# The MoE output product as three split products, with the low half of w2 made on GpSimd

## The reference

```
def expert_block(args):
    xb, e = args
    return (jax.nn.silu(xb @ exp_w1[e]) * (xb @ exp_w3[e])) @ exp_w2[e]
```

## Time and profile before

| | |
|---|---|
| time, median of 3 | 3186.52 us (3183.03 to 3187.85) |
| the profiled execution | 3187.85 us, its span 3185.8 us |
| busy over the span | PE 88%, PEld 59%, DVE 43%, ACT 33%, POOL 18% |
| stage 6 | from about 2215 us to the end |
| output product L2072 | 736 records, 323.6 us busy |
| hidden products L2042 | 2208 records, five groups, 904.8 us busy |
| low parts of w1 and w3, L1850 | 256 on VectorE, 296.2 us busy |
| high parts of w1 and w3, L1909 | 256 on ScalarE, 248.9 us busy |

### The profile page before, as it was taken

How to read it: one execution, slowest core, us unless ns; L and a number is a source line. 1 busy time by engine, 2 the same in 40 slices (tenths; PEclk the granted TensorE clock), 3 DMA queues, 4 the chain that set the end, 5 groups by cost and what they waited for, 6 DMA issues and landing times. The chain is left out here.

```text
span 3185.8 us, 38331 instructions
## 1 busy us (share of the span) xinstructions
PE 2792.0 (88%) x11587; PEld 1871.8 (59%) x11588; DVE 1355.5 (43%) x2342; ACT 1049.3 (33%) x2001; POOL 578.5 (18%) x1206
## 2 busy tenths in 40 slices
PE   5985999999949777797999999981799999999998
PEld 1334644444435554556899999971566666666655
DVE  4655375221203232233255444521465465544564
ACT  3226121111112212122255555420444454433452
POOL 0000011000000000005145455554121121211232
PEclk9995999999979888895599999975899999999999
DMA  7455111121178787854011111101687698666694
GB/s 293 145 138 183 29 42 40 40 66 36 31 191 238 182 205 181 209 124 128 17 59 61 63 53 53 49 34 46 229 307 233 199 342 286 230 224 201 216 327 132
DMA packets 305306, 466.75 MB, mean 147 GB/s; under 512 B 27048, under 2 KB 193600, under 8 KB 298336
## 3 DMA queue, kind: packets, MB, share of 16 engines
q1 hardware_dynamic: 223410, 384.14, 38.1%
q0 software_dynamic: 16976, 39.52, 5.5%
q10 hardware_dynamic: 64832, 41.96, 4.7%
HBM read 367.33 MB, written 113.81 MB: 151 GB/s over the span
## 5 line engine op out<-in xcount | busy, mean ns | idle before, releaser
L748 PE MATMUL ps_proj<-sb_hT,sb_win 128*128 128x512 f32 x768 | 335.5, 596 | 7.6 <-DVE sb_rot L837 6.0
L2072 PE MATMUL ps_byp<-sb_w,sb_gT 128*128 128x512 f32 x736 | 323.6, 592 | 0.7 <-ACT sb_gT L1926 0.7
L2042 PE MATMUL ps_bh<-sb_w,sb_bxTh 128*128 128x512 f32 x736 | 295.4, 401 | 0.0
L748 PEld LDWEIGHTS ps_proj<-sb_hT,sb_win 128*128 128x128 f32 x768 | 145.6, 191 | 189.5 <-issue 182.6
L2072 PEld LDWEIGHTS ps_byp<-sb_w,sb_gT 128*128 128x128 f32 x736 | 136.2, 190 | 154.9 <-issue 154.0
L1620 DVE CUSTOM_DVE_ANT_0 sb_pr<-ps_S,sb_mask 128x640 f32<-128x640 f32 x128 | 105.6, 825 | 216.4 <-PE ps_S L1469 216.3
L1138 DVE TENSOR_TENSOR sb_ab<-sb_ab,ps_prod 128x512 f32<-128x512 f32 x64 | 44.1, 689 | 358.5 <-ACT sb_ab L1114 358.5
L2042 PE MATMUL ps_bh<-sb_w1h,sb_bxTh 128*128 128x512 f32 x368 | 164.0, 446 | 26.0 <-DVE sb_w L1850 17.3
L1489 PE MATMUL ps_O<-sb_v,sb_pt 128*128 128x64 f32 (+1 forms) x1280 | 175.9, 293 | 0.0
L1489 PEld LDWEIGHTS ps_O<-sb_v,sb_pt 128*128 128x128 f32 x1280 | 173.2, 214 | 0.0
L1341 POOL MEMSET sb_pr<- 128x1026 int32 x1 | 1.0, 958 | 909.5 <-POOLq L185 909.5
(11 more groups left out here) (274 smaller groups left out, 5179.4 us busy)
## 6 DMA issues: line engine op xcount, KB each, us to landing
sb_raw_w<-in_exp_w SPq DMA_DIRECT2D x60, 2048.0 KB, 13.0
sb_w<-in_exp_w SPq DMA_DIRECT2D x30, 2048.0 KB, 8.1
sb_ada<-in_ada_w SPq DMA_DIRECT2D x16, 1536.0 KB, 7.4
scr_filt<-sb_fout ACTq DMA_DIRECT2D x128, 128.0 KB, 2.5
sb_yh<-scr_filt SPq DMA_DIRECT2D x32, 512.0 KB, 11.1
scr_hy_y<-sb_sp SPq DMA_DIRECT2D x32, 512.0 KB, 11.5
sb_yx<-scr_hy_y SPq DMA_DIRECT2D x32, 512.0 KB, 7.9
scr_hy_v<-sb_yx SPq DMA_DIRECT2D x64, 256.0 KB, 4.2
```

The source lines that it names most:

```text
L748: ins = pe.matmul(mp[:, (NQ + n) % 4, :], w[:, pc % 3, k, (ct % 2) * P:(ct % 2 + 1) * P], g.hT[:, k, c * 512:(c + 1) * 512], start=(k == 0 ...
L2042: ins = pe.matmul(out, a[:, k, :], b(k), start=(k == 0 and j == 0), stop=(k == n - 1 and j == 2))
L2072: ins = pe.matmul(yp[:, half, :], gT[:, k, :], w2[par][:, k, cs], start=(k == 0), stop=(k == FT - 1))
```

## The change

The output product takes the split form too.

- w2 is loaded into a raw tile. Two casts of 128x2048 on ScalarE (`high2`) make its high part `w2h`, behind Silu in each first block. Two subtractions of 128x2048 on GpSimd make the low part, written over the raw one, between the scatter and the gather of a first block.
- The gated tile is cast to its high part `gTh` on ScalarE (`gated_high`, where the copy was), and VectorE subtracts to get the low part (`gated_low`), ahead of its gating multiplication.
- TensorE's `output` calls `split_product`: 24 products in place of 8. It waits for the low parts instead of the copy and the load.
- To make room, the high part of w3 is in one buffer instead of two. ScalarE therefore waits, ahead of its casts for a first block, until the hidden products of the block before are done.

```diff
-        w2 = [e.sb(st, f"w2_{b}", [P, FT, D]) for b in range(2)]
+        raw2, w2 = zip(*[raw_and_low(f"w2_{b}", [P, FT, D]) for b in range(2)])
-        w3h = [e.sb(st, f"w3h_{b}", [P, KT, FH], F32R) for b in range(2)]
+        w3h = e.sb(st, "w3h", [P, KT, FH], F32R)
+        w2h = [e.sb(st, f"w2h_{b}", [P, FT, D], F32R) for b in range(2)]
...
@@ VectorE
+            def gated_low(n):
+                ve.wait_ge(ghi, n)
+                ve.tensor_tensor(cols(gT), cols(gp), cols(gTh).bitcast(F32), ALU.subtract).then_inc(glo, 1)
+
             def body(n, ex, par, half, first):
                 if first:
                     low13(ex, par, 1)
+                if not starts(n):
+                    gated_low(n)
...
@@ ScalarE
+            def high2(par, half):
+                act.wait_ge(ldw2[par], 16 * (half + 1))
+                for part in range(2):
+                    cs = slice(part * (FT * D // 2), (part + 1) * (FT * D // 2))
+                    act.copy(cols(w2h[par])[:, cs], cols(raw2[par])[:, cs]).then_inc(hi2, 1)
...
                 if first:
+                    if not starts(n):
+                        act.wait_ge(hm, 2 * n + 1)
                     high13(ex, par, half, 1)
...
                 act.activation(sg[:, :], hp[:, 0, :], ACT.Silu).then_inc(sgd, 1)
+                if first:
+                    high2(par, half)
                 turned(n + 1)
...
@@ GpSimd
                 scatter(n)
+                if first:
+                    for part in range(2):
+                        pool.wait_ge(hi2, 2 * ex + part + 1)
+                        pool.sem_inc(passed, 1)
+                        cs = slice(part * (FT * D // 2), (part + 1) * (FT * D // 2))
+                        pool.tensor_tensor(cols(w2[par])[:, cs], cols(raw2[par])[:, cs],
+                                           cols(w2h[par])[:, cs].bitcast(F32), ALU.subtract).then_inc(lo2, 1)
                 gather(n + 2)
...
@@ TensorE
-                pe.wait_ge(gtc, n + 1)
+                pe.wait_ge(glo, n + 1)
...
-                    for k in range(FT):
-                        ins = pe.matmul(yp[:, half, :], gT[:, k, :], w2[par][:, k, cs], start=(k == 0), stop=(k == FT - 1))
-                    ins.then_inc(ym, 1)
+                    split_product(yp[:, half, :], gTh, gT, lambda k: w2h[par][:, k, cs], lambda k: w2[par][:, k, cs], FT)\
+                        .then_inc(ym, 1)
...
-                    if first:
-                        pe.wait_ge(ldw2[1 - par], 16 * (half + par))
-                    else:
-                        pe.wait_ge(ldw2[par], 16 * (half + 1))
+                    pe.wait_ge(lo2, 2 * ex if first else 2 * ex + 2)
```

More of the change, by code:

```diff
@@ L1736, in stage6 @@
         sg = e.sb(st, "sg", [P, FH])
-        gT = e.sb(st, "gT", [P, FT, P])
+        gT = e.sb(st, "gT", [P, FT, P], F32R)
+        gTh = e.sb(st, "gTh", [P, FT, P], F32R)
         y = e.sb(st, "by", [P, D])
@@ L1749, in stage6 @@
         lo13 = e.sem("s6_w13_low")
+        hi2 = e.sem("s6_w2_high")
+        lo2 = e.sem("s6_w2_low")
         rl = e.sem("s6_records_loaded")
@@ L1761, in stage6 @@
         gtt = e.sem("s6_gated_turned")
-        gtc = e.sem("s6_gated_turned_copied")
+        ghi = e.sem("s6_gated_high")
+        glo = e.sem("s6_gated_low")
         ym = e.sem("s6_output_product")
@@ L1808, in high @@
         def high(par, m):
-            return w3h[par] if m else w1h[par]
+            return w3h if m else w1h[par]
         def cols(t, m=None):
@@ L1820, in load2 @@
             src = i["exp_w2"][0, bass.ds(ex, 1)].rearrange("a (k p) f -> p (a k) f", p=P)
-            eng.dma_start(w2[par][:, :, :], src).then_inc(ldw2[par], 16)
+            eng.dma_start(raw2[par][:, :, :], src).then_inc(ldw2[par], 16)
         @block.vector
@@ L1843, in _ @@
             ve.tensor_copy(info[:, 1, :], inf[:, 1, :]).then_inc(cnt, 1)
+            ve.sem_inc(glo, 1)
             def low13(ex, par, m):
@@ L1900, in _ @@
             total = experts(ve, body)
+            gated_low(total)
             output(total)
@@ L1922, in turned, with gated_high @@
                 act.copy(cols(xTh)[:, 512:], cols(xf)).then_inc(xhi, 1)
-            def gated_copied(n):
+            def gated_high(n):
                 act.wait_ge(gtt, n)
-                act.copy(cols(gT), cols(gp)).then_inc(gtc, 1)
+                act.copy(cols(gTh), cols(gp)).then_inc(ghi, 1)
             def body(n, ex, par, half, first):
@@ L1930, in body @@
                 if first:
+                    if not starts(n):
+                        act.wait_ge(hm, 2 * n + 1)
                     high13(ex, par, half, 1)
                 if not starts(n):
-                    gated_copied(n)
+                    gated_high(n)
                     act.wait_ge(gd, n)
@@ L1951, in _ @@
             total = experts(act, body)
-            gated_copied(total)
+            gated_high(total)
         @block.gpsimd
@@ L2059, in turn_gated @@
                 pe.wait_ge(gd, n)
-                pe.wait_ge(gtc, n)
+                pe.wait_ge(glo, n)
                 for f in range(FT):
@@ L2087, in body @@
                 if not starts(n):
-                    if first:
-                        pe.wait_ge(ldw2[1 - par], 16 * (half + par))
-                    else:
-                        pe.wait_ge(ldw2[par], 16 * (half + 1))
+                    pe.wait_ge(lo2, 2 * ex if first else 2 * ex + 2)
                     pe.sem_inc(passed_t, 1)
                     output(n, 1 - par if first else par)
-            for s in (hm, ym, gtc):
+            for s in (hm, ym):
                 pe.sem_inc(s, 1)
@@ L2099, in _ @@
             turn_gated(total)
-            pe.wait_ge(ldw2[1], 16 * (NE // 2))
+            pe.wait_ge(lo2, 2 * NE)
             output(total, 1)
```

## The result

| | median us | lowest to highest |
|---|---|---|
| before | 3186.34 | 3183.03 to 3187.85 |
| after | 3212.59 | 3210.64 to 3214.81 |

The account below looks back on a forecast made before the run. TensorE bounds the stretches alternating first and second blocks; first-block runs also wait for VectorE. Runs +46.1, alternating -12.3 and ends -1.8 make +32 on 3187.85, 3219.9; adjusted to the median, 3218.5 us, own range 3198 to 3240, stated range 3147 to 3240.

Parts of the forecast that it names:

- rival B: VectorE in stage 6: no exclusion when GpSimd is first, so the halves are hidden; 3149 us, chance 0.22.
- Output product, 1.15 us less a block: TensorE, stage 6: 24 split products replace 8 fp32 ones, and the next hidden product shortens; 19.33 becomes 18.2 us.
- Casts hidden, w2 landed in time: ScalarE behind Silu: two w2 casts of about 1.95 us run from 7.6 to 11.6, inside 5.44 us idle.
- rival D: ScalarE: w2 lands late, casts end at 17 instead of 11.6 and hold later work; +18, 3237 us, chance 0.09.
- Low part 4.51 us a half, gather and TensorE not held up by it: GpSimd, between scatter and gather: 9.0 us per expert, hidden from the gather and from TensorE's use next block.
- Full exclusion with GpSimd first: Shared SBUF port: a running GpSimd half holds VectorE's two-SBUF-input instructions; second L1864 piece ends at 19.45, due at 16.4.
- The copy of the earlier trace as nearest row: One-column GpSimd copy meeting VectorE's four L1850 subtractions took 4.25 us, not 0.18; taken as evidence for full exclusion.
- Rival C: Exclusion, but a waiting VectorE slips in between the two GpSimd halves: about -15, 3203 us, chance 0.12.
- Chain of a first block behind a first block: Consecutive blocks each first using a new expert's weights: late VectorE and halves give 23.4 us (14 cases) or 21.5 (four).
- the slow product: TensorE's first hidden product after a wait: clock 0.65, 8.4 us instead of 6.0, moving the next block to 23.8.
- Rival E: VectorE slowed, not stopped: the hold costs about what the product gives back; 3186 us, chance 0.05.
- Sum: Stage 6 total: runs of first blocks +46.1, alternating stretches -12.3, end blocks -1.8; together +32 us.

Follow-up runs that it names:

- the writes alone: Changed kernel, but GpSimd fills the low part of w2 with zeros, reading no SBUF, instead of subtracting: 3148.7 us, ratio 0.988.
- the cost alone: Kernel before, with one w3h buffer and the change's ScalarE casts and GpSimd subtractions added on scratch tiles nothing reads: 3236.7 us, ratio 1.015.
- the first experiment: Changed kernel, with GpSimd writing zeros as w2's low part instead of subtracting, so it reads no SBUF: 3148.7 us, ratio 0.988.
- The early copy: Changed kernel, but GpSimd copies the scatter's row numbers before it waits for the output tile: 3201.29 us, ratio 1.0039.

## Why the prediction was right

The forecast of 3218.5 is 6 us above the measured median, and its mechanism is the one that the runs show. The stated range alone, 3147 to 3240, would prove little: it takes in a kernel that is no slower, and rival B's 3149. The blocks and the experiments carry the argument. Point by point, with what the runs made of each:

- *Output product, 1.15 us less a block.* Right: 5.66 us was the forecast for the product; between 2826.35 and the next first product lie 6.79, of which 0.96 is wait, so 5.83 with the end of the last product. Second blocks fell to 18.1.
- *Casts hidden, w2 landed in time.* Right. The two take 3.72 us (3.9 was the estimate). ScalarE waited 1.5 us in all for w2 ahead of these casts, so rival D was not there. (The load of the earlier trace rows takes 8.1, not 8.2.)
- *Low part 4.51 us a half, gather and TensorE not held up by it.* Right: median 4.62, and the only late user was VectorE.
- *Full exclusion with GpSimd first.* This was the step on which the sign hung, and no row of before showed it. The 2.99 us and the writes alone show it, and the cost alone agrees. In the Trainium skill's rule ("SBUF — State Buffer", "Who interferes with whom") the part that no row of before could show was the one that decided; both orders are seen now (4.25 us for the copy, 2.99 for the piece), and its exception for a GpSimd instruction that only writes holds in the first experiment (0.68).
- *The copy of the earlier trace rows as nearest row.* It was read as if it stood for all. In stage 6 of the kernel before, 13 such copies fall on VectorE's four low parts of w3. Nine take 4.25 us; four, at 2353.26, 2633.34, 2655.67 and 3109.16, get in behind the first of the four, as this one, which ends at 2354.32, just behind VectorE's first part (2354.28):

```profile
2353.26 1.06 POOL L1976 COPY sb_rows_out<-sb_brec 128x1 int32 x1 [13.64 <-DVE sb_by L1875]
...
2353.05 4.63 DVE L1850 TENSOR_TENSOR sb_w<-sb_raw_w,sb_w3h 128x1024 fp32r<-128x1024 f32 x4
```

  So "did not get in" was one of two outcomes, and what decides between them the traces don't tell. The forecast needed less: that the second half, once begun, holds one VectorE instruction to its end. That was borne out; the argument for it read more into the row than the rows beside it allow.
- *Rival C (VectorE slips in between the halves).* Its case did not come up in the changed kernel: in every block with halves the second piece of L1870 starts after the first half has ended, so it always met the second half alone. With the casts ahead of Silu, where VectorE was waiting as the first half ended, it did get in.
- *Chain of a first block behind a first block.* The time was right, 23.3 for 23.4. The reason was weighted wrongly: I put the late start of the halves on the scatter's copy first (23.05) and on the slow product second (23.8). The early copy took away the first and gained 11 us, not 27. The 22.5 that is left stands against 21.1 in a block of that kernel whose first product ran at full clock. So the slow product, seen behind 15 of the 18 waits of the changed kernel, is the larger of the two: up to 1.5 us a block against 0.8. That 23.4, the middle of two cases, was met to 0.1 is luck in part. One such block:

```profile
2604.71 0.77 PE L2072 MATMUL ps_bh<-sb_w1h,sb_bxTh 128*128 128x512 f32 x1 [4.41 <-DVE sb_w L1856]
...
2616.88 9.21 POOL L2012 TENSOR_TENSOR sb_w<-sb_raw_w,sb_w2h 128x2048 fp32r<-128x2048 f32 x2 [1.14 <-ACT sb_w2h L1928]
```

- *Rival B (no exclusion), 3149.* It is the time of the kernel in which GpSimd only writes, 3148.7: the gain side of the sum had the right size. Rival E, a hold worth what the product gives back, falls by the same number: the reads cost about 63 us and the product gives 38 to 40.
- *Sum.* Runs +43.6 for +46.1, alternating -16.0 for -12.3, the ends -2.1 for -1.8. The second term was 3.7 us short, 3 of it because each isolated first block was put at 19.5 and took 19.2: the halves start at 9.3 there, not at 9.7.

## What to carry to other kernels

When work is given to an idle GpSimd, ask which VectorE instructions with two SBUF inputs will run beside it, and whether one of them stands on the path to TensorE; busy shares (here 45% and 29%) say nothing of it. If it can't be moved away, cut GpSimd's instructions small or split them so that they end ahead of that point: the same change went from 0.8% slower to 0.7% faster by small pieces alone, and to 1.0% faster shared between the engines (and with the early copy); the two are not clear of each other. Small pieces are no guarantee: once, eight of them in a row held VectorE for 4.01 us. Look for the hold in an instruction's duration, not in the waits.

## What I had not expected of the hardware

- A run of instructions can keep the other engine out or let it in by turns. With VectorE's four subtractions running, a 0.18 us copy took 4.25 us in nine cases and about 1.1 in four. A GpSimd half that came upon the same four got in behind the second, and from there the two engines took turns: 13.41 us for the four. What decides isn't shown.
- Waits of TensorE of nearly the same length (2.7 to 2.8 us) were followed by a first product at a granted clock of 1.00 (5.6 us) or of 0.64 (8.4 us), in the same execution. In the fast one all products run at the upper of the two levels, 2.4 GHz, 0.23 us apart; in the slow one most of the time is spent at the lower, 1.2 GHz, 0.43 us apart.
